# A two-block transformer kernel: whole-width first products in two feed-forwards, unread products after an expert stage, and the band mask moved into the bias product

## The reference, cut to what matters

```python
def conv_ffn(h, w_in, conv_w, conv_b, w_out):
    u = h @ w_in                      # 1024 -> 5632
    ...
    a, b = jnp.split(u, 2, axis=-1)
    return (jax.nn.silu(a) * b) @ w_out

def swa_sink_mixer(h, k, v, w_q, sinks, bias, mask, w_out):
    ...
    logits = logits + bias.astype(jnp.float32).reshape(SW_KV_HEADS, SW_GROUP, SW_WINDOW, 2 * SW_WINDOW)
    logits = jnp.where(mask[None, :, None, None], logits, -jnp.inf)
    ...

for layer in range(DEPTH):
    ...                               # mix = the layer's mixer of h
    h = layer_norm_2(ALPHA_2 * h + mix, ln_mix_g[layer], ln_mix_b[layer])
    ff = conv_ffn(h, ffn_w_in[layer], ffn_conv_w[layer], ffn_conv_b[layer], ffn_w_out[layer])
    h = layer_norm_2(ALPHA_2 * h + ff, ln_ffn_g[layer], ln_ffn_b[layer])
```

## Time and profile before

| | us |
|---|---|
| median of 3 runs | 1408.45 |
| lowest and highest of them | 1407.83, 1408.49 |
| the profiled execution, whole | 1409.36 |
| its span in the trace | 1407.6 |
| PE busy in it | 1326.5 |
| DVE, ACT, POOL busy | 758.9, 548.5, 118.5 |
| mean granted clock of PE, share of full | 0.977 |

### The profile page before, as it was taken

How to read it: one execution, slowest core, us unless ns; L and a number is a source line. 1 busy time by engine, 2 the same in 40 slices (tenths; PEclk the granted TensorE clock), 3 DMA queues, 4 the chain that set the end, 5 groups by cost and what they waited for, 6 DMA issues and landing times.

```text
span 1407.6 us, 20789 instructions
## 1 busy us (share of the span) xinstructions
PE 1326.5 (94%) x8168; PEld 973.4 (69%) x8168; DVE 758.9 (54%) x1432; ACT 548.5 (39%) x996; POOL 118.5 (8%) x131
## 2 busy tenths in 40 slices
PE   8989999999798999999979898999999988999997
PEld 7767444343686744344459786699997874999985
DVE  3976212112688631111264795687775655478766
ACT  5554111111446321121144232166654453366552
POOL 1030000000003100000030450310000021000000
PEclk9999999999899989999989999999999999999999
DMA  9439899999724779999995239745765510555740
GB/s 308 148 119 369 353 420 421 421 420 395 243 76 180 309 320 420 421 420 421 421 335 180 90 120 120 235 131 181 245 225 185 182 60 1 190 186 186 248 148 30
DMA packets 130136, 347.83 MB, mean 247 GB/s; under 512 B 10288, under 2 KB 86342, under 8 KB 105476
## 3 DMA queue, kind: packets, MB, share of 16 engines
q1 hardware_dynamic: 125232, 332.29, 62.7%
q0 software_dynamic: 3952, 13.74, 4.3%
q10 hardware_dynamic: 868, 0.63, 0.1%
HBM read 342.44 MB, written 4.19 MB: 246 GB/s over the span
## 4 chain that ended last, share of the span: by engine, by line
PE 75%; DVE 12%; DMA 4%; SPq 4%; ACT 2%; issue 2%; POOL 0%; DVEq 0%; ACTq 0%
PE bank L1938 11%; PE bank L1769 8%; PE bank L1771 8%; PE bank L1770 8%; PE bank L1949 6%; PE bank L1673 5%; SPq L642 4%; DMA slot<-in_w_up 4%; PE bank L1781 4%; PE bank L2256 3%; PE bank L2260 3%; PE bank L2258 3%; PE bank L2139 2%; PE bank L1713 1%; PE bank L1960 1%
## 5 line engine op out<-in xcount | busy, mean ns | idle before, releaser
L1769 PE MATMUL bank<-x_high,w_high 128*128 128x256 f32 x1024 | 291.1, 284 | 2.3 <-DVE w_low L1213 2.3
L1770 PE MATMUL bank<-x_low,w_high 128*128 128x256 f32 x1024 | 289.7, 283 | 0.0
L1771 PE MATMUL bank<-x_high,w_low 128*128 128x256 f32 x1024 | 289.7, 283 | 0.0
L774 ACT ACTIVATE w_high<-slot 128x1024 fp32r<-128x1024 f32 x214 | 215.5, 1054 | 183.7 <-PE bank L1771 86.2
L1938 PE MATMUL bank<-slot,arena 128*64 128x512 f32 x976 | 223.0, 592 | 1.5 <-DMA slot<-in_w_up 1.5
L1769 PEld LDWEIGHTS bank<-x_high,w_high 128*128 128x128 f32 x1024 | 196.5, 192 | 4.5 <-issue 4.4
L1770 PEld LDWEIGHTS bank<-x_low,w_high 128*128 128x128 f32 x1024 | 196.5, 192 | 0.1
L1771 PEld LDWEIGHTS bank<-x_high,w_low 128*128 128x128 f32 x1024 | 196.5, 192 | 0.0
L1938 PEld LDWEIGHTS bank<-slot,arena 128*64 128x64 f32 x976 | 73.3, 137 | 142.5 <-issue 142.2
L1570 DVE TENSOR_TENSOR w_low<-slot,w_high 128x1024 fp32r<-128x1024 f32 x88 | 103.8, 1222 | 61.3 <-ACT w_high L774 61.0
L774 ACT ACTIVATE arena<-bank 128x512 f32<-128x512 f32 (+7 forms) x130 | 60.4, 495 | 167.1 <-PE bank L2023 85.1
(11 more groups left out here) (299 smaller groups left out, 2216.7 us busy)
## 6 DMA issues: line engine op xcount, KB each, us to landing
slot<-in_w_gate SPq DMA_DIRECT2D x62, 1024.0 KB, 19.6
slot<-in_w_up SPq DMA_DIRECT2D x60, 1024.0 KB, 18.9
slot<-in_w_down SPq DMA_DIRECT2D x60, 1024.0 KB, 18.7
slot<-in_ffn_w_in SPq DMA_DIRECT2D x44, 1024.0 KB, 7.6
slot<-in_ffn_w_out SPq DMA_DIRECT2D x22, 1024.0 KB, 5.0
slot<-in_hgrn_w_in SPq DMA_DIRECT2D x16, 1024.0 KB, 7.0
slot<-in_w_in SPq DMA_DIRECT2D x10, 1024.0 KB, 9.8
slot<-in_w_o SPq DMA_DIRECT2D x8, 1024.0 KB, 5.0
```

Of the source, the lines that this page charges most:

```text
L774: return nc.scalar.activation(dst, src, ACT.Copy)
L1769: mm(dst, high[:, k, :], x_high[:, k, :], start=(k == 0), stop=False)
L1770: mm(dst, high[:, k, :], x_low[:, k, :], start=False, stop=False)
L1771: last = mm(dst, low[:, k, :], x_high[:, k, :], start=False, stop=(k == KD - 1))
```

## The change

In words:

- `next_x`: PE no longer transposes tile 0 inside the projection. Both tiles are transposed after `y11`, with 7 unread products of 256 columns on PE between them (`FILL`, `busy_half`) and 1 ahead of the transposes of the convolution's weights, which now come first. Then `U00` and `U01` are done whole, 256 tokens wide; in `U00`'s a part the kinds "h" and "w" come ahead of "x".
- `norm` on DVE no longer interrupts itself: all four `low_tokens` follow the whole of it.
- `experts`: 8 unread products of 256 columns follow the last `scatter`, in both layers.
- Layer 1's mixer: the high half of `f1` is copied on ACT ahead of the tokens, its low half on DVE right behind the norm, and `ikdk` does its "h" and "w" matmuls before it waits for the low tokens. Layer 0 gets the same order in `ikdk`. Where `xT` is made too, ACT takes the second root ahead of tile 0's `x_high`.
- The band becomes a 33rd row of the selection matrix, with ones as 33rd row of the table (a memset on POOL). The transfer of the band and POOL's addition are gone; DVE waits for the skewed rows instead.

The diff, cut to its core:

```diff
+    pick = np.concatenate([pick, np.where((d >= 0) & (d < P), 0.0, NEG).astype(np.float32)[None, :]])
...
+            pool.memset(rel[NBUCKET:NBUCKET + 1, :], 1.0).then_inc(sem("rel_one"), 1)
-            pool.dma_start(F["band"], io["c_band"]).then_inc(sem("band_in"), 16)
...
-            pool.wait_ge(sem("skew_in"), 32)
-            pool.wait_ge(sem("band_in"), 16)
-            nc.gpsimd.tensor_tensor(F["bias"], F["bias"], F["band"].unsqueeze(1).to_broadcast([P, SWQ, NK]), ALU.add).then_inc(sem("bias_ready"), 1)
...
             def transposed_split(k, l, y, whole=False):
+                for t in range(NT):
+                    if k is not None and (t == 0 or not whole):
+                        std_of(k, t)
+                    if whole:
+                        copies(t, xT, "x_whole")
+                    if k is not None and whole and t == 0:
+                        std_of(k, 1)
+                    copies(t, x_high, "x_high_ready")
...
             def mixer(l):        # ACT
-                split_first(l)
+                split_first(l, [1] if l else range(2))
...
                 if l == DEPTH - 1:
                     split_slot(2, "hq0", HG_UNIT)
+                else:
+                    split_first(l + 1, [0])
...
             def norm(k, l, y, from_psum):     # DVE
-                        if t and h and low_between is not None:
-                            low_tokens(l, y, low_between, [0])
...
             def mixer(l):        # DVE
+                if l:
+                    low_first(l, [0])
                 low_tokens(*((l - 1, "m") if l else (0, "in")), l)
-                low_first(l)
+                low_first(l, [1] if l else range(2))
...
             def feed_forward(l): # DVE
-                low_tokens(l, "y", 2 * (l - DEPTH) + 3, [1])
+                low_tokens(l, "y", 2 * (l - DEPTH) + 3)
...
-            dve.wait_ge(sem("bias_ready"), 1)
+            dve.wait_ge(sem("skew_in"), 32)
...
+            FILL = {("y", 1): 7}
+
             def transpose_tile(l, y, t, ready):
+                if (y, t) in FILL:
+                    busy_half(reuse(pe, (l, f"{y}xT{t}1")), FILL[(y, t)])
...
+            def busy_half(b, n):
+                for _ in range(n):
+                    mm(b[:, 0:T], ident[:, :], ident[:, :].unsqueeze(1).to_broadcast([P, 2, P]), start=True, stop=True)
...
             def mixer(l):        # PE
                 b = narrow(l, 1)
+                pe.wait_ge(sem("split"), 2 * IN_UNIT[l] + 1)
+                pe.wait_ge(sem("x_high_ready"), 4 * (l + 1))
+                for k in range(KD):
+                    mm(b[:, T:2 * T], w_high[0][:, 0, k, :], x_high[:, k, :], start=(k == 0), stop=False)
+                    mm(b[:, T:2 * T], w_low[0][:, 0, k, :], x_high[:, k, :], start=False, stop=False)
                 transposes_out(*((l - 1, "m") if l else (0, "in")))
-                pe.wait_ge(sem("split"), 2 * IN_UNIT[l] + 1)
-                done(split_product(b[:, T:2 * T], w_high[0][:, 0, :, :], w_low[0][:, 0, :, :]), (l, "ikdk"))
+                for k in range(KD):
+                    last = mm(b[:, T:2 * T], w_high[0][:, 0, k, :], x_low[:, k, :], start=False, stop=(k == KD - 1))
+                done(last, (l, "ikdk"))
...
                 scatter(PAIRS - 1)
+                busy_half(reuse(pe, (l, "mxT01")), 8)
...
             def next_x(l, y, k):
+                for t in range(NT):
+                    transpose_tile(l, y, t, normed(k))
                 b = reuse(pe, (l, "cw"))
                 pe.wait_ge(sem("cw_in"), 48 * (l - 1))
+                busy_half(b, 1)
...
+                b = reuse(pe, (l, "U00"), 0)
                 pe.wait_ge(sem("x_high_ready"), before_x + 4)
+                for ab in range(2):
+                    pe.wait_ge(sem("split"), 2 * n + ab + 1)
+                    passes(b, n, ab, "hw", first=True)
+                    if ab == 0:
+                        transposes_out(l, y)
+                    last = passes(b, n, ab, "x", last=True)
+                done(last, (l, "U00"))
+                b = reuse(pe, (l, "U01"), 0)
+                for ab in range(2):
+                    pe.wait_ge(sem("split"), 2 * (n + 1) + ab + 1)
+                    last = split_product(b[:, T * ab:T * (ab + 1)], w_high[1][:, ab, :, :], w_low[1][:, ab, :, :])
+                done(last, (l, "U01"))
```

66 lines of the change are left out of this document (17 added, 49 removed).

## The result

The changed kernel took 1400.16 us in the median of four runs (1399.41 to 1401.45), against 1408.47 for the kernel before (1407.83 to 1410.26): a ratio of 0.994, 95% interval 0.9927 to 0.9953. That is 8.3 us faster where 12.3 were forecast, and 0.16 us outside the range of the prediction. The direction was right, the size was not.

A forecast was written before the change was run, and what follows sets the result against it. The prediction took PE, busy 94%, to bound the kernel, with a wait for DVE at layer 1's mixer. Gains of 11.0 (both feed-forwards) + 1.3 (mixer) = 12.3 us took 1408.45 to 1396.1, range 1391.4 to 1400.0.

The forecast's parts named there:

- Part 1: Begins of layer 2's and 3's feed-forwards: whole products save PE 9.8 us against a new wait; gain 5.5 us each.
- The third unit and POOL: Layer 2's feed-forward: with POOL's band addition kept, the third unit's split would come 4 us late; moving it avoids this.
- Case (d): Rival: the third unit's split or its weights come late, 1 to 2 us each; 1398 to 1400; chance 0.08.
- Case (c): Rival: clock falls in the gap ahead of the first units, losing 3.35 us each; 1399.5 to 1402.8; chance 0.12.
- case (e): Rival, the other side: half clock through the first units, whole products 0.24 us apart, makes it slower, 1419; chance 0.02.
- The rule of the Trainium skill: At both feed-forward begins: transposes do not count as PE being busy like matmuls, so the clock can fall there.
- Part 2: Begin of layer 1's mixer: the first wide product starts at 370.40 instead of 371.70, gaining 1.3 us.
- The second root: Layer 1's mixer begin: taken earlier on ACT so tile 1's norm ends earlier; no gain while the half clock stays.
- Part 3: Fill of eight unread products behind the last scatter: taken as no gain, up to 1.6 us lost per layer.
- Case (b): Rival: the unread products behind the last scatter hold the clock, 1.7 + 2.8 us more gained; 1391.6; chance 0.12.

## Why the prediction was wrong

**Part 1, the feed-forward begins.** Right, step by step: 5.4 and 5.46 us where 5.5 each were written. The half of the columns really costs nearly the same as the whole, and the chain is 6.1 us long. The row of layer 2 in the last table is 0.6 short; it also takes in the half-clock stretch ahead of the begin, which falls on other work there. In the totals the kernel with these begins and the band alone is 11.0 us below before (means of 5 and 63 runs).

**The third unit and POOL.** Right: without the band's move the split comes late and the gap is 3.43 us, where "4 us late" was written for the split. The kernel with the band on POOL shows that nearly all of part 1 in layer 2 hangs on the band's move: of 4.9 us 0.5 are left. That the move gives nothing by itself was not tried, and the 0.6 us in layer 3's mixer speak against it. Case (d) did not occur.

**Case (c).** Right in its weighing: the unread products hold the clock, and without them it falls in both begins, for 2.4 and 1.0 us where case (c) had 3.35 each. A whole product at half clock starts 0.21 us behind the last, not the 0.24 of case (e), so the other side was priced too high. The rule of the Trainium skill (TensorE: Matmul & The Clock Gate, Part 4: PE-mode transpose), which I set against the change, did not decide: the clock was at full over tile 1's transposes and the units behind them in all three traces. Whether transposes alone would have held it, no run here shows.

**Part 2, the mixer's begin.** The mechanism was right and its size too small: 1.7 to 1.8 us at the place in place of 1.3. Of the difference 0.25 is that the first wide product doesn't wait for the narrow product's modelled end, which my sum had as its start. The other 0.2 is less than the spread between traces of one cell. The second root, of which I wrote that nothing comes, may have a part in it: with the fill tile 1's rows follow tile 0's after 4.7 to 5.3 us in place of 5.9 and 6.3, without it after 4.4 in place of 4.9 and 5.0. But without the fill the last narrow product starts 10.1 to 10.4 us behind the rows, against 10.05 and 10.9 in the old order, which shows no gain of the root's. In the total none of the part's gain is shown.

**Part 3, the fill: the step that failed.** "I take nothing", with up to 1.6 us of loss by half clock as the bound. It costs 1.9 to 2.0 us at layer 1's begin and eats the mixer's gain there, so that this begin gave 0.2 to 0.4 us in place of 1.3. 1.6 of it is the later start of tile 0's transposes, which is not the clock's doing; the other 0.3 to 0.4 goes with the half-clock stretch, which then lies 3 us further on. I asked how long the products run (3.7 us, done well ahead of the transposes: also right) and not what they stand in front of in PE's program: a register load and a branch, behind which PE goes on only after 6.4 to 6.6 us where it has to wait. In the trace of before the branch starts 6.12 us ahead of the transposes, so at most some tenths of the idle time ahead of them were spare, and the branch was held back by 1.2 us. Case (b), that the fill gives clock back, was wrong in its price: with the fill the mean granted clock is higher by 0.003 and the stretches at the end of layer 1 are shorter, but no time is saved. "Nothing" is what the totals show of the fill, within 1.3 us either way; that is luck as far as my reasons go.

**The sum.** With the two terms as measured at the place, 10.9 + 1.8 - 1.95, it is 10.7 us, or 1397.7 against the median of before. The mean difference over all runs is 10.2, between 9.0 and 11.4 if all runs are independent. The forecast of 12.3 lies outside that, though one of the three sets, with 12.4, met it; the time that the mean gives, 1408.45 - 10.2 = 1398.2, lies inside the range. The same sum fails without the fill: it gives 10.9 + 1.8 = 12.7, and the eleven runs lie 10.1 us below before (9.2 to 10.9). So the fill explains the 1 us missing at layer 1's begin in the changed kernel's traces. It doesn't explain the total, since the shortfall stays when the fill is gone; what takes it there is open.

**The range.** The 1400.16 of the first measurement is 1.4 us above the mean of all fifteen. No mechanism found here accounts for that, and I take it as scatter. My range took in unknown costs and left out that one program's runs spread over 6 us, because the three runs that I had lay within 0.7 us. The trace of before showed the reason for doubt: of two equal routers one had run at half clock. Why this first set lay high as a whole, all four runs at 1399.4 or more, stays open; only one of the four has a trace.

## What to carry to other kernels

Ahead of a branch, idle time of an engine is not all free: find the branch in the trace, add the time until the engine goes on behind it, and see whether a filler holds the branch back. An unread product pays where it bridges a gap right ahead of dense work that would else start at half clock, and a filled gap is worth only what work stands behind it. Look for equal pieces of work at unequal clocks in one trace before giving a range: their difference is part of the scatter of the total, however close together the first few runs lie. And check that what is won at one place reaches the end: here 1.7 us won and 1.9 us lost in layer 1 both left the total where it was.

## What the runs showed of the hardware

In all seventeen traces a 16 KB transfer on the instruction queue starts 3.7 to 4.0 us behind PE's branch at the end of layer 0, and where PE has to wait it goes on 6.4 to 6.6 us behind the branch. That this is code being fetched is inferred from the queue's name and from the kernel with 224 more instructions. Whether the branch itself takes 0.4 or 6.2 to 6.4 us is a matter of 8 instructions more ahead of it, or of 224 more, which put it right again. A small DVE operation of 0.16 us took 12.61 us beside a POOL addition of 13.46 us and ended with it. Three microseconds of idleness ahead of the first units brought the clock down in both layers, and a gap of 3.43 us inside dense products did so too.
